# Two column tiles of a split projection multiplied together while a norm delivers its input tiles

## What is computed

```python
h = layer_norm(DN_ALPHA * x + m, ln1_g[i], ln1_b[i])
f = jnp.square(jax.nn.relu(h @ mlp_w1[i])) @ mlp_w2[i]
e = jax.nn.sigmoid(h @ ple_w_gate[i]) * (p[i] @ ple_w_proj[i])
...
y = xf * lax.rsqrt(jnp.mean(xf * xf, axis=-1, keepdims=True) + EPS)
h_l = modulate(x, norm1_g[layer], mod_l, 0)
... jnp.split(h @ w_in, bounds, axis=-1)
... sq_relu_mlp(modulate(x, norm2_g[layer], mod_l, 3), mlp_w1[layer], mlp_w2[layer])
```

## Time and profile before

| | us |
|---|---|
| median of 3 runs | 3435.7 (3434.79 to 3443.48) |
| the profiled execution | 3433.8 |
| its span, first to last instruction | 3431.6 |
| TensorE busy | 3221.9 (94% of the span) |
| VectorE busy | 1581.9 (46%) |
| ScalarE busy | 1218.6 (36%) |
| mean granted TensorE clock | 0.96 of full speed |

### The profile page before, as it was taken

The page is one execution under the profiler, slowest core; times in us unless marked ns, Lnnn a source line. Parts: engine busy times, 40 slices in busy tenths (PEclk is TensorE's granted clock), DMA queues, the critical chain, the costliest instruction groups (busy, mean ns, idle before and its releaser), DMA issues. The chain is left out here.

```text
span 3431.6 us, 39333 instructions
## 1 busy us (share of the span) xinstructions
PE 3221.9 (94%) x15200; PEld 2503.1 (73%) x15200; DVE 1581.9 (46%) x2389; ACT 1218.6 (36%) x2022; POOL 79.3 (2%) x84
## 2 busy tenths in 40 slices
PE   7798999999899899998998998899999997999999
PEld 6575677773477577775885787788888774768887
DVE  3754466671144476665423633333233424344444
ACT  2344233332364333335213453422322324543332
POOL 4100000000000000000000200000000000000000
PEclk9959999999999999998999999899999989999999
DMA  4201343431311234431121000111212110012221
GB/s 161 75 1 49 123 169 149 165 126 18 56 55 50 81 145 154 171 147 32 51 61 49 1 1 25 50 53 69 73 49 73 49 50 25 1 69 88 89 96 74
DMA packets 160792, 259.36 MB, mean 76 GB/s; under 512 B 58476, under 2 KB 73194, under 8 KB 160556
## 3 DMA queue, kind: packets, MB, share of 16 engines
q1 hardware_dynamic: 158932, 252.94, 20.9%
q10 hardware_dynamic: 1628, 4.76, 0.3%
q0 software_dynamic: 128, 0.26, 0.0%
HBM read 255.85 MB, written 2.10 MB: 75 GB/s over the span
## 5 line engine op out<-in xcount | busy, mean ns | idle before, releaser
L1172 ACT ACTIVATE w_hi<-wbuf 128x1024 fp32r<-128x1024 f32 x330 | 348.4, 1058 | 1246.5 <-PE psA L750 1197.1
L748 PE MATMUL psA<-act_hi,w_hi 128*128 128x512 f32 (+1 forms) x1824 | 701.0, 384 | 62.9 <-DVE act_lo L1783 42.5
L749 PE MATMUL psA<-act_lo,w_hi 128*128 128x512 f32 (+1 forms) x1824 | 685.5, 376 | 0.0
L750 PE MATMUL psA<-act_hi,w_lo 128*128 128x512 f32 (+1 forms) x1824 | 685.0, 376 | 0.0
L1777 DVE TENSOR_TENSOR w_lo<-wbuf,w_hi 128x1024 fp32r<-128x1024 f32 x330 | 404.1, 1228 | 561.4 <-ACT w_hi L1172 556.6
L748 PE MATMUL psA<-hid_hi,w_hi 128*128 128x512 f32 (+1 forms) x1280 | 476.8, 372 | 3.1
L749 PE MATMUL psA<-hid_lo,w_hi 128*128 128x512 f32 (+1 forms) x1280 | 471.9, 369 | 0.0
L750 PE MATMUL psA<-hid_hi,w_lo 128*128 128x512 f32 (+1 forms) x1280 | 471.2, 368 | 0.0
L748 PEld LDWEIGHTS psA<-act_hi,w_hi 128*128 128x128 f32 x1824 | 350.5, 192 | 149.5 <-issue 52.6
L749 PEld LDWEIGHTS psA<-act_lo,w_hi 128*128 128x128 f32 x1824 | 351.6, 193 | 60.5 <-issue 3.6
L750 PEld LDWEIGHTS psA<-act_hi,w_lo 128*128 128x128 f32 x1824 | 350.4, 192 | 61.4
(11 more groups left out here) (230 smaller groups left out, 3567.3 us busy)
## 6 DMA issues: line engine op xcount, KB each, us to landing
wbuf<-in_mlp_w_dram SPq DMA_DIRECT2D x64, 2048.0 KB, 7.9
work<-in_ada_w_dram SPq DMA_DIRECT2D x32, 1536.0 KB, 10.9
wbuf<-in_ab_w_in_dram SPq DMA_DIRECT2D x10, 1024.0 KB, 5.0
wbuf<-in_ple_w_gate_dram SPq DMA_DIRECT2D x4, 2048.0 KB, 7.6
wbuf<-in_hy_w_in_dram SPq DMA_DIRECT2D x3, 2048.0 KB, 7.7
wbuf<-in_c_w_in_dram SPq DMA_DIRECT2D x3, 2048.0 KB, 7.5
wbuf<-in_hy_w_out_dram SPq DMA_DIRECT2D x2, 2048.0 KB, 7.8
wbuf<-in_mla_w_out_dram SPq DMA_DIRECT2D x2, 2048.0 KB, 7.9
```

The lines of the kernel that those rows point to most:

```text
L748: pe.matmul(psA[:, s, a:b], w_hi, x_hi[:, a:b], start=first, stop=False)
L749: pe.matmul(psA[:, s, a:b], w_hi, x_lo[:, a:b], start=False, stop=False)
L750: ins = pe.matmul(psA[:, s, a:b], w_lo, x_hi[:, a:b], start=False, stop=last)
L1172: return nc.scalar.activation(out, in_, func, **kw)
```

## The change

TensorE's list alone is changed. Where a wait on the activation tiles is given, the first two units are multiplied by a new `split_pair`: it waits for w_lo of both units once, and calls `split_products` for both slots of psA, with the k tiles 0, 1, 2, 3, 4 each as a piece of its own and 5, 6, 7 as the last piece. Within a piece all of unit 0 is done (512 columns, then 256 if there are any), then all of unit 1. The later units are as before. In the MLP this holds for mlp2 and mlp3 only (`name not in ADA`; mlp0 and mlp1 are as before): there group 0 is written out ahead of the loop, and the loop runs groups 1 to 7.

```diff
+            def split_pair(stage, n, x_hi, x_lo, wait):
+
+                def operands(j, k):
+                    return split_place(wH, stage, j)[:, k, :], split_place(wL, stage, j)[:, k, :], x_hi[:, k, :], x_lo[:, k, :]
+
+                pe.wait_ge(S["w_split"], BASE_W[stage] + 2)
+                split_products(stage, [0, 1], n, operands, halves=[range(k, k + 1) for k in range(KD - 3)] + [range(KD - 3, KD)],
+                               wait=wait)
+
             def split_linear(stage, x_hi, x_lo, n, wait=None, units=KD, behind=None, first=0):
-                for u in range(first, units):
+                if wait:
+                    split_pair(stage, n, x_hi, x_lo, wait)
+                for u in range(2 if wait else first, units):
                     pe.wait_ge(S["w_split"], BASE_W[stage] + u + 1)
                     hi, lo = split_place(wH, stage, u), split_place(wL, stage, u)
-                    split_products(stage, [u], n, lambda j, k: (hi[:, k, :], lo[:, k, :], x_hi[:, k, :], x_lo[:, k, :]),
-                                   wait=wait if u == 0 else None)
+                    split_products(stage, [u], n, lambda j, k: (hi[:, k, :], lo[:, k, :], x_hi[:, k, :], x_lo[:, k, :]))
...
             def mlp(name, index, n):
-                with pe.Fori(0, GROUPS) as i:
+                def group(i, paired):
                     more = i * ((GH + KD) // 2)
-                    for u in range(GH):
+                    if paired:
+                        split_pair(name, n, sH[n], sL[n], split_here(name))
+                    for u in range(2 if paired else 0, GH):
...
+                paired = name not in ADA
+                if paired:
+                    group(0, True)
+                with pe.Fori(1 if paired else 0, GROUPS) as i:
+                    group(i, False)
```

## The result

| | us |
|---|---|
| changed kernel, median of 4 runs | 3414.64 (3412.91 to 3416.37) |
| kernel before, median of 4 runs beside it | 3435.24 (3434.61 to 3443.48) |
| ratio | 0.9939, 95% interval 0.9926 to 0.9952 |
| the profiled execution; its span | 3412.91; 3410.7 |
| forecast | 3409.2, range 3401 to 3425 |

The time lies inside the range and 5.4 us above the forecast: 20.6 us were saved where the sum said 26.5.

What follows compares the result with a forecast made beforehand. TensorE, 94% busy, was taken as the bound, losing time to waits for VectorE's lo tiles and, more, to half clock. 24.8 + 7.1 - 5.4 = 26.5 us saved gave 3407.3, plus 1.9 for the median 3409.2 us; range 3401 to 3425.

Steps and rivals of the forecast that it cites:

- the sum: Whole kernel: 24.8 us and 7.1 us saved, 5.4 us lost, so 26.5 us faster.
- Step (1): ab, mlp2, c_k: two units in hand leave no pauses, the clock rises, each pair takes 19.2 us; 24.8 us saved.
- the low clock the larger part: TensorE in ab and mlp2: half clock for 15.6 and 18.5 us called a larger part than the waits.
- The forecast on waits: TensorE's waits for lo tiles fall by less than a third; the rest of the gain is clock.
- Step (2): ple_g0, ple_g1, mlp3: pairs shorten, but unit 2 waits for unit 0's reading or w_lo; 7.1 us saved together.
- Step (3): hy_xr, hy_out, mla_out, c_out, ab_out: no gain, new holes before unit 2, ab_out starts later; 5.4 us lost.
- Step (4): Group 0 of mlp2 and mlp3 ahead of the loop: entry costs 0 to 6.2 us each, taken as 0.
- Step (5): Alternating psA's slots from tile to tile: price already in the 1.05 us per tile; no weight-load cover gets thinner.
- the slower rival: Six norm pairs: taking slots in turn keeps the clock low; 31.8 us slower, 3467 us; chance 0.04.
- The late clock: ab, mlp2, c_k: clock returns only when all tiles have arrived; 9.6 us saved in all, 3426 us; chance 0.07.
- the loop stall: Loop entry in mlp2 and mlp3 stalls up to 6.2 us twice; 3415 to 3422 us; chance 0.05.
- Gain lost further on: Weight load or barrier comes last instead of TensorE: half lost 3422 us, chance 0.07; all lost 3435 us, 0.03.

Runs made afterwards that it cites:

- The filled kernel: Against the kernel before: no pairs; three extra matmuls after each of unit 0's first seven tiles in ab, mlp2, c_k; group 0 ahead of loop; 3434.45 us.
- the norm stages alone: Against the changed kernel: only ple_g0, ple_g1, ab, mlp2, c_k and mlp3 paired, the five copy-fed stages unit by unit; 3407.32 us.
- The five stages alone: Against the kernel before: only hy_xr, hy_out, mla_out, c_out and ab_out paired; 3445.48 us, ratio 1.0024.
- the second set: The changed kernel run again as the same program, all eleven stages paired, nothing changed; 3411.38 us, ratio 0.9934 to the kernel before.

## Why the prediction came out as it did

**Step (1), the 768-token pairs: right.** 19.2 us forecast, 19.21, 19.23 and 19.21 measured, and 24.2 us by the experiment with these three alone against 24.8. Both of its bounds are seen: in ab the work at full clock plus the half-clock start, since TensorE has no pause there, and in mlp2 and c_k the last tile's arrival. The clock is at half for 3.5 us in mlp2 and c_k (0.09 x 2 x 19.2) and 5.0 in ab, inside the 3.4 to 5.8 that I took from four other starts.

**What I said of it was too simple in one place.** I called the low clock the larger part, as if it could be had by itself. The filled kernel has the full clock from 4.6 us on in mlp2 and gains 3.8 of 24.8 us. What the pairs bring is unit 1's work laid under the arrivals; the full clock is the condition for 16.8 us of work to fit there (by the sum's own prices; pairs at a low clock weren't run). The sum didn't use the sentence, so the number didn't suffer. The forecast on waits (less than a third gone) was right, 12.1 of 51.4 us.

**Step (2), the 512-token norm pairs: the mechanism right, a size off.** Forecast 13.9, 13.9 and 13.1 us; measured 15.16 in ple_g0, 1149.12 - 1135.18 = 13.94 in ple_g1, and 14.04 in mlp3. The mis-sized term is the half-clock start: 6.0 us in ple_g0 and 5.2 in mlp3, against 3.8 and 3.4. Put into the prediction's own formulas, 10.9 + 0.47 x 6.0 - 2.04 + 3.3 = 15.0 and 10.9 + 0.47 x 5.2 - 2.04 + 2.67 = 14.0. I had read each stage's start time from the one profile as if it belonged to the stage; it belongs to the execution (ple_g0: 3.4 us before, 6.0 after, 3.4 with the norm stages alone). The 3.8 us of the prediction were a small misreading besides: at a granted clock of 0.55, 0.45 x 2 x 3.8 = 3.4 us of them are at half clock. The gain was 0.9 + 2.1 + 2.0 = 5.0 us instead of the 7.1 forecast.

**Step (3), the copy-fed stages: right in kind, the size not settled.** The holes are 0.38, 1.12, 1.12, 0.48 and 1.18 us against 0.6, 1.2, 1.2, 0.55 and 1.25. ab_out starts 1.1 us later as the rows of VectorE and TensorE show, the counterpart of the earlier trace rows:

```profile
2090.76 2.35 DVE L1795 TENSOR_TENSOR w_lo<-wbuf,w_hi 128x1024 fp32r<-128x1024 f32 x2
...
2093.17 0.79 PE L748 MATMUL psA<-act_hi,w_hi 128*128 128x512 f32 x1 [7.54 <-DVE w_lo L1795]
```

The wait is 7.54 us, before it was 6.40. The five stages alone cost 8.7 us by the medians, and leaving them out is worth 4.1 or 7.3. By those three numbers their price is 4 to 9 us, with the forecast 5.4 among them. Beyond the holes the one profile has it in stretches at a lower granted clock, and kernels without these pairs show the same there; a cause that ties it to the pairs isn't shown.

**Step (4), the loop entry: right at 0.** Group 1 starts 0.12 us after group 0's last matmul in mlp2 and 0.23 us after it in mlp3, the distances that matmuls of that size have anywhere. The rule of the Trainium skill that the prediction named (Runtime: NRT & Kernel Launch, Instruction fetch mechanics) didn't cost anything measurable at these two entries; whether the branch's target was already fetched there, no row tells.

**Step (5), slots in turn: right.** All of the pairs reach granted clock 1.00 with alternating slots, so the slower rival is refuted. The rule that the prediction weighed beside it (the Trainium skill, TensorE: Matmul & The Clock Gate, A second HAM failure mode: psum-queue depth-cycling) doesn't show here.

**The rivals.** The late clock is refuted by the 15.88 us at 1.00 in mlp2, the loop stall by the two entries just named. Gain lost further on: not in the sense meant. Stretches without a change, mlp0 to mla_out and mlp1 to ab, changed by between 0.7 us gained and 2.1 us lost, in both signs.

**The 5.4 us between forecast and median.** Some of it is noise: the second set's median is only 2.2 us above the forecast. By the second execution's column, in which the clock stayed full behind hy_v, 3.7 us are missing: 1.3 in mlp3, 2.6 in the two unchanged stretches, and the rest evens out, which is luck: c_k's stretch gained 1.1 us more than the sum gave it and ab's 0.9 less. In mlp3 the pair took 14.18 us where the sum had 13.1. So in that execution about a third is the mis-sized half-clock start, and the rest differences in stretches that nothing edits. Subtracting from one profiled execution presumes that its unchanged stretches are typical. The profile of before was a fortunate one in at least the first stretch: every other profile, those with hy_xr unpaired too, reaches hy_out 0.4 to 6.1 us later than its 262.85, and behind hy_yr its clock was 0.75, where it is 0.73 in two of the others and 0.68 or 0.69 in seven, with hy_xr paired or not. The changed kernel again:

```profile
95.61:263.24 167.63, 148.16 (x528) 0.68 0.07 26
```

Adding 1.9 us for the median covered part of that.

## What to carry to other kernels

Where an engine is fed at intervals by a slower one, count the work that it has in hand between two arrivals: once two units bridge the interval, the pauses and the low clock go together. Here the clock alone was worth little, and the order alone is estimated to be. Pairing ends the first unit late, so whoever reads it or waits for its slot is uncovered by as much; leave a tail of unit-by-unit tiles that is about as long as the longest reading, if the arrivals allow it, and leave stages alone in which nothing has to be waited for. Take the lengths that a clock needs to come back as a range over executions and not one value for each stage.

## What the hardware showed beyond that

The time at half clock after a start is not fixed by the stage: in the six norm pairs of one execution it was 3.5 to 6.0 us, and in ple_g0's pair 6.0 in the changed kernel and 3.4 in the one with the norm stages alone. These are windows in the changed kernel that are wholly at half clock, in ple_g0 and mlp3:

```profile
337.23:343.25 6.02, 6.02 (x14) 0.50 0.00 0
3044.82:3050.02 5.20, 5.20 (x12) 0.50 0.00 2
```

And a stretch of small matmuls with short pauses (12.5 us busy of 15.7) ran at full clock in nine profiles and fell to half for 13.7 us in the tenth, which made 4.7 us of difference. One of the nine is another execution of the same program. A pause of 2.53 us was followed by half clock in ple_g0 and by full clock in ple_g1, in one execution.
